# One network on one core: fewer product chunks between the transposes that open the channel-decay scan

## What is computed

```python
def rwkv7_scan(r, w, k, v, kk, a):      # inputs (B, L, H, N): L = 256, H = 16, N = 64
    def step(state, xs):
        r_t, w_t, k_t, v_t, kk_t, a_t = xs
        sa = jnp.einsum('bhvk,bhk->bhv', state, -kk_t)
        state = (state * w_t[:, :, None, :] + sa[..., None] * (kk_t * a_t)[:, :, None, :]
                 + v_t[..., None] * k_t[:, :, None, :])
        return state, jnp.einsum('bhvk,bhk->bhv', state, r_t)
    ...
# then, in rwkv7_branch: a norm per head, weight and bias, + bonus * v, * silu(z)
```

## Time and profile before

| | |
|---|---|
| median of 3 runs | 2408.6 us (2404.01 to 2412.79) |
| the profiled execution | 2403.41 us, span 2401.6 us |
| PE busy | 2238.3 us (93%) |
| DVE / ACT / POOL busy | 1585.6 (66%) / 1070.5 (45%) / 115.2 us (5%) |
| chain that ended last | PE 72%, DVE 14%, DMA 6%, ACT 4%, issue 3% |
| mean granted clock of PE | 0.981 |

### The profile page before, as it was taken

One profiled execution on the slowest core, in us unless ns is written; L12 is line 12 of the kernel. 1 busy time (PEld: TensorE's weight loads), 2 busy tenths in 40 slices (PEclk: granted clock), 3 DMA queues, 4 the chain that ended last, 5 costly groups with the idle time before them and its releaser, 6 DMA issues.

```text
span 2401.6 us, 35278 instructions
## 1 busy us (share of the span) xinstructions
PE 2238.3 (93%) x14268; PEld 1840.7 (77%) x14268; DVE 1585.6 (66%) x2362; ACT 1070.5 (45%) x1490; POOL 115.2 (5%) x188
## 2 busy tenths in 40 slices
PE   7999889999999999999999989888899989989997
PEld 6889678887878788877777767776677777767876
DVE  5665675558894546659999675665955556567754
ACT  5444565445444655553333653233444323244443
POOL 0000001010001001000000100001010000011000
PEclk9999999999999999999999999999999999989999
DMA  7666338667687449775554734249676333477753
GB/s 232 189 192 203 99 117 298 225 193 247 234 290 283 154 155 334 239 254 195 185 189 152 249 111 155 84 135 338 231 288 217 125 109 114 139 275 237 244 188 124
DMA packets 222594, 481.67 MB, mean 201 GB/s; under 512 B 14880, under 2 KB 51536, under 8 KB 217696
## 3 DMA queue, kind: packets, MB, share of 16 engines
q1 hardware_dynamic: 200112, 372.91, 47.2%
q0 software_dynamic: 22320, 106.51, 12.1%
HBM read 421.97 MB, written 57.40 MB: 200 GB/s over the span
## 4 chain that ended last, share of the span: by engine, by line
PE 72%; DVE 14%; DMA 6%; ACT 4%; issue 3%; POOL 0%; SPq 0%; ACTq 0%; POOLq 0%; DVEq 0%
PE mm_acc L291 59%; DVE mm_lo L208 3%; DMA mm_raw<-in_w_in 2%; ACT mm_hi L201 2%; PE s_bu L2819 1%; PE s_y L2832 1%; DMA rwk_src<-rw_rh 1%; DVE gdn_cv L1829 1%; DMA in_xt<-proj 1%; PE in_turn L374 1%; PE rwk_bank L2343 0%; DMA in_xt<-x 0%; DMA in_xt<-in_x 0%; DMA rw_v<-rwp_ft 0%; DVE s5t_tab L2718 0%
## 5 line engine op out<-in xcount | busy, mean ns | idle before, releaser
L208 DVE TENSOR_TENSOR mm_lo<-mm_raw,mm_hi 128x1024 fp32r<-128x1024 f32 (+4 forms) x672 | 791.9, 1185 | 525.6 <-ACT mm_hi L201 516.3
L201 ACT CAST mm_hi<-mm_raw 128x1024 fp32r<-128x1024 f32 (+4 forms) x672 | 681.8, 1019 | 862.2 <-PE mm_acc L291 827.2
L291 PE MATMUL mm_acc<-mm_hi,mm_aT_hi 128*128 128x512 f32 (+5 forms) x2208 | 880.3, 399 | 40.7 <-DVE mm_lo L208 35.5
L291 PE MATMUL mm_acc<-mm_hi,mm_aT_lo 128*128 128x512 f32 (+5 forms) x2208 | 852.0, 386 | 0.0
L291 PE MATMUL mm_acc<-mm_lo,mm_aT_hi 128*128 128x512 f32 (+5 forms) x2208 | 851.3, 386 | 0.0
L291 PEld LDWEIGHTS mm_acc<-mm_hi,mm_aT_hi 128*128 128x128 f32 x2208 | 421.6, 191 | 134.5 <-DVE mm_lo L208 48.0
L291 PEld LDWEIGHTS mm_acc<-mm_hi,mm_aT_lo 128*128 128x128 f32 x2208 | 420.8, 191 | 77.5
L291 PEld LDWEIGHTS mm_acc<-mm_lo,mm_aT_hi 128*128 128x128 f32 x2208 | 422.0, 191 | 67.5 <-issue 1.0
L291 PE MATMUL mm_acc<-mm_hi,in_yT_hi 128*128 128x512 f32 x256 | 101.7, 397 | 3.0 <-DVE mm_lo L208 3.0
L291 PE MATMUL mm_acc<-mm_hi,in_yT_lo 128*128 128x512 f32 x256 | 100.5, 393 | 0.0
L291 PE MATMUL mm_acc<-mm_lo,in_yT_hi 128*128 128x512 f32 x256 | 100.4, 392 | 0.0
(11 more groups left out here) (635 smaller groups left out, 2155.6 us busy)
## 6 DMA issues: line engine op xcount, KB each, us to landing
mm_raw<-in_w_in SPq DMA_DIRECT2D x384, 512.0 KB, 5.4
mm_raw<-in_w_out SPq DMA_DIRECT2D x96, 512.0 KB, 5.2
mm_raw<-in_w_in SPq DMA_DIRECT2D x72, 464.0 KB, 4.1
mm_raw<-in_w_branch SPq DMA_DIRECT2D x48, 512.0 KB, 5.3
proj<-mm_stage SPq DMA_DIRECT2D x46, 512.0 KB, 3.1
mm_raw<-in_w_in SPq DMA_DIRECT2D x32, 416.0 KB, 4.9
home_tab<-s5t_tab POOLq DMA_DIRECT2D x4, 2048.0 KB, 9.6
s_tab<-home_tab POOLq DMA_DIRECT2D x8, 1024.0 KB, 5.9
```

Source lines behind the costliest of these rows:

```text
L201: self.nc.scalar.copy(self.hi[:, c % RING, :, 0:t.w], self.raw[:, c % RAW, :, 0:t.w]).then_inc(self.hi_done, 1)
L208: self.nc.vector.tensor_tensor(self.lo[:, c % RING, :, 0:t.w], self.raw[:, c % RAW, :, 0:t.w], self.hi[:, c % RING, :, 0:t.w].bitcast(F32) ...
L291: last = nc.tensor.matmul(self.acc[s][m][:, 0:t.w], t.aT[a][:, k, m * P:(m + 1) * P], b[:, c % RING, k - k0, 0:t.w], start=(k == 0 and fir ...
```

## The change

In the front, a point follows each fourth job (after jobs 3, 7, 11 and 15) instead of each one. The phase has 108 points instead of 120, and still 72 chunks, so each point gets 2/3 of a chunk instead of 3/5.

```diff
-        pace = Pace(mm, n_all, 10 + len(jobs) + NQ * (4 + INVERSE_POINTS + 6) + 6)
+        pace = Pace(mm, n_all, 10 + len(jobs) // 4 + NQ * (4 + INVERSE_POINTS + 6) + 6)
...
                 for j in range(len(jobs)):
                     turner.copy(act, jobs[j:j + 1])
-                    pace.act(act)
+                    if j % 4 == 3:
+                        pace.act(act)
...
                 for j in range(len(jobs)):
                     turner.turn(pe, jobs[j:j + 1])
-                    pace.pe(pe)
+                    if j % 4 == 3:
+                        pace.pe(pe)
...
-                pace.dve(dve, 10 + len(jobs))
+                pace.dve(dve, 10 + len(jobs) // 4)
```

## The result

The changed kernel takes 2420.96 us (median of 6 runs, 2417.91 to 2422.92), the kernel before 2408.98 us (6 runs, 2404.01 to 2412.79): **slower by 0.45%, ratio 1.0045, 95% interval 1.0035 to 1.0056**. The forecast was 2418, range 2409 to 2427, with a chance of 0.66 for slower. Sign, range and size came out; of the terms of the sum two were clearly wrong, in opposite directions (the wait before job 12 and the clock in the rounds).

A forecast was written before the change was run, and what follows sets the result against it. PE was taken as nearly full in the front, with holes in the rounds. Front -7.2, six chunks +17.4, waits -1.3 and clock +0.5 gave +9.4 us, beside the median 2418 us, range 2409 to 2427.

The forecast's parts named there:

- the wait before job 12: In the front, PE waits 3.5 us for the second `al` and `rh`, whose transfer was taken at 7.9 us.
- the clock in the rounds: In the four rounds, one fall of PE's clock fewer was held possible: -0.8 us.
- The front: From the first transposes to P1: 25.6 us, 35.1 before, so P1 of round 0 starts 9.5 us earlier.
- The wait before job 4: In the front, PE waits 4.3 us for the first `al` and `rh`, where it waited 2.3 before.
- The rival of the early transfer: Second transfer lands early, with SP's loads held, or waits are better covered: no measurable change, 2414 us; chance 0.18.
- The late first mask: Start of round 0: first mask 3.6 us behind P1, PE's wait before the second P1 about 4.5 us.
- Kept by the second P1: Of the front's 9.5 us gain, 7.2 us remain at the second P1 of round 0.
- Six chunks at 2.9 us: From the second P1 on, PE has six more chunks to do: +17.4 us.
- The waits give almost nothing back: In the rounds, PE's waits return 1.2 of 17.4 us, 1.3 with short unlisted gaps.
- The pricing by places: Each empty point in the rounds costs what the same place cost before; round starts 1 to 3 gain 0.2 us.
- The clock: Falls of PE's granted clock: +1.3 us in the front, -0.8 in the rounds, +0.5 in the sum.
- The low-clock rival: Clock stays low through the turned jobs and into round 0: +13.4 us, 2422 us; chance 0.12.

The follow-up runs named there:

- e4: Changed kernel with thrown-away matmuls in four of PE's long waits (before job 4 and three in the rounds): 2409.23 us, ratio 1.0010 to the kernel before.
- e2: Changed kernel with DVE's three memsets ahead of the front's three low parts instead of behind them: 2415.10 us, ratio 1.0033 to the kernel before.
- e5: Kernel before, same chunk counts in front and rounds, with each round's chunks placed at points where PE waited: 2398.81 us, ratio 0.9960.
- e6: Changed kernel with its 59 chunks in the rounds placed at chosen points, the front unchanged: 2399.25 us, ratio 0.9957 to the kernel before.
- e7: Kernel before with thrown-away matmuls in four of its waits in the rounds, no chunk moved: 2399.71 us, ratio 0.9971.
- e8: Changed kernel with four waits filled by thrown-away transposes in place of matmuls: 2414.11 us, ratio 1.0027 to the kernel before.

## Why the prediction came out, step by step

- **The front** (25.6 us forecast from the first transposes to P1): 26.0. But by other parts. The wait before job 4 was forecast at 4.3 and was 4.07. The wait of 3.5 before job 12 didn't exist: the transfer took 4.5 us, not 7.9. The rival of the early transfer had this right, and also its cause, that SP's loads are held then. As an estimate by the Trainium skill ("DMA: Bandwidth & Descriptors", Anatomy of one DMA) I had worked out 4.4 us for both halves; this trace has 5.0 from the first issue to the last landing. In place of the 3.5 us stood three other things: job 4 started 11.1 us behind the first transposes and not 9.7 (1.4), the half clock over the turned jobs cost 1.7 (against e4), and three waits for ACT between jobs 8 and 15 made 0.8. A wait of 2.1 for `ka`, where I had at most 0.9 together with the bank, delayed nothing, since the long wait stood behind it. That the sum of these is 26.0 is luck: the same front took 21.6 to 25.6 in five other profiles.
- **The late first mask:** forecast 4.5 us of wait and 9.7 from P1 to P1; measured 4.33 and 9.5. e2 confirms the cause. Kept by the second P1: 7.2 forecast, 7.0 measured in this pair.
- **Six chunks at 2.9 us:** about right as PE's work. Of the 22.3 us by which PE's busy time rose, 17.4 were forecast for the chunks, and the 4.9 left over is near the 5.6 that half of the additional 11.2 us at half clock would be. From e5 to e6 the time at half clock goes the other way (13.7 to 6.8 us) and busy time rises by 13.2, which is again some 2.8 a chunk. (The prediction's "62 chunks" from the second P1 to the end of the rounds count the four behind the rounds too; it is 58 there, before 52.)
- **The waits give almost nothing back** (1.3): measured nothing, 22.4 and 22.5 us idle. The pricing by places held for the masks (3.4, 1.3 and 2.1 us in rounds 1 to 3, where I had 3.4, 1.3 and 2.2). L1450 waited 3.46 in round 2 as forecast, but 1.83 in round 1, where I had 0.5; that alone is the 1.3.
- **The clock, the step that failed by size.** I put +1.3 on the front and -0.8 on the rounds. It is +1.7 in the front (from job 4 on, against e4) and about +5 in the rounds (4.9 to 5.6, above). I had forecast one fall fewer in the rounds. There were six and the end of a seventh in place of five, and single ones lasted 6.8 us, not 3.4. e4 and e7 show that these stretches cost about half their length. The low-clock rival had the mechanism, though not the place: I looked for it in the front, and more of it was in the rounds.
- So in this pair the rounds cost 7.1 us more than forecast, 5.7 of it the clock and the rest the waits, and the front kept 1.1 more than forecast, which has 1.3 for its clock: 9.4 + 7.1 - 1.1 = 15.4. The medians show 12.0 and the ratio 10.8, nearer to the forecast of 9.4 than this one pair. The granted clock of all runs gives up to 7.6 us for the clock, where the sum has 0.5. Part of the agreement is luck: what the front gives back beyond the forecast, 1.9 us on average over the profiles, hides part of what the rounds cost beyond it.

What stays open: when a wait under 3 us brings a fall, and why single falls last 6.8 us and others 3.4; and the 1.6 to 3.2 us waits on "issue" inside the inverse, which move from place to place between kernels.

## What to carry to other kernels

Background work is worth moving only into a place where the bounding engine waits: list the waits of the stage that receives it, and lay the empty slots against that list one by one, since an even spread puts most of it where nothing waits. Read the granted clock beside the waits. On PE a wait can be paid twice, once as idle time and again as a stretch at half clock behind it: in this phase the waits of 2.9 us and more all were, those of 2.1 to 2.7 us only in part. Work that is thrown away can be cheaper than the wait. And one profile is not enough for the length of a stage: the same front took 21.6 to 26.0 us. Look also what stands behind the last moved piece on the helping engines, here three memsets.

## What was new about the hardware

- Thrown-away matmuls in four waits made the kernel before faster by 0.29% (0.17 to 0.41) and the changed one by about 0.35%, though the chain that PE waits for got no shorter: from P1 to the second P1 it took 7.4 us with and without them in the kernel before, 9.6 and 9.5 in the changed one.
- Thrown-away transposes held the granted clock too: 1.00 through the front of e8, with 32 of them in the wait before job 4, where three profiles with 4.1 us of empty wait fell to 0.50.
- A wait of 2.32 us at one and the same place was followed by full clock in the kernel before and by 3.4 us at half clock in e5.
- A stretch at half clock slows transposes too: jobs 4 to 7 took 3.76 us in it and 2.47 at full clock, with the same copies between them.
- Half a megabyte landed 4.5 us after issue with no other loads beside it (4.4 to 5.7 in the nine profiles with this front), and 7.9 us after issue with SP's loads beside it (7.2 and 8.0 in e5 and e7).
